# Second norm of a hybrid decoder layer: the gain applied to turned rows by VectorE in halves, the stored rows scaled by ScalarE

## The reference, cut to what matters

```python
def rmsnorm(x, g):
    xf = x.astype(jnp.float32)
    xf = xf * lax.rsqrt(jnp.mean(xf * xf, axis=-1, keepdims=True) + EPS)
    return xf.astype(x.dtype) * g

x = x + merged @ lp['w_out']                      # this is h
x = x + hier_moe(rmsnorm(x, lp['norm2_g']), lp)   # the second norm
...
# hier_moe: router logits from xt, top-1 of 4 groups, then top-2 of 8 experts inside it
for e in range(N_EXPERTS):                        # 32 experts, 1024 -> 256 -> 1024
    h = jax.nn.silu(xt @ lp['w_e_gate'][e]) * (xt @ lp['w_e_up'][e])
    y = y + combine[:, e:e + 1] * (h @ lp['w_e_down'][e])
```

## Time and profile before

| what | value |
|---|---|
| three runs, us | 781.94, 782.52, 783.98; median 782.52 |
| profiled execution | span 783.6 us; its own time outside the span is not on the page |
| PE busy | 741.4 us, 95% |
| VectorE busy | 408.8 us, 52% |
| ScalarE busy | 259.2 us, 33% |
| POOL busy | 74.4 us, 9% |
| moved by DMA | 190.68 MB, mean 243 GB/s |
| mean granted clock of PE | 0.990 |

### The profile page before, as it was taken

How to read it: one execution, slowest core, us unless ns; L and a number is a source line. 1 busy time by engine, 2 the same in 40 slices (tenths; PEclk the granted TensorE clock), 3 DMA queues, 4 the chain that set the end, 5 groups by cost and what they waited for, 6 DMA issues and landing times.

```text
span 783.6 us, 12757 instructions
## 1 busy us (share of the span) xinstructions
PE 741.4 (95%) x5288; PEld 576.0 (74%) x5288; DVE 408.8 (52%) x755; ACT 259.2 (33%) x446; POOL 74.4 (9%) x104
## 2 busy tenths in 40 slices
PE   8999999999999999999999999999999997778884
PEld 7999999999999777899999988885333332323322
DVE  6999839986347785665154386554112111114226
ACT  5662351123486645532442341230111111100113
POOL 0100022001011111000000000011121221111100
PEclk9999999999999999999999999999999999999997
DMA  9578326434238433400260694389999999999994
GB/s 342 202 264 316 109 82 106 118 115 151 102 131 323 162 138 118 182 1 2 108 219 12 222 425 189 128 353 345 419 423 424 418 424 424 419 423 425 422 388 161
DMA packets 38143, 190.68 MB, mean 243 GB/s; under 512 B 5914, under 2 KB 7466, under 8 KB 21864
## 3 DMA queue, kind: packets, MB, share of 16 engines
q1 hardware_dynamic: 23696, 148.22, 47.8%
q0 software_dynamic: 11200, 34.98, 13.4%
q10 hardware_dynamic: 3184, 6.60, 2.3%
HBM read 176.17 MB, written 21.41 MB: 252 GB/s over the span
## 4 chain that ended last, share of the span: by engine, by line
PE 76%; DMA 14%; DVE 5%; ACT 3%; issue 1%; SPq 1%; DVEq 0%; ACTq 0%; POOLq 0%
PE ps L662 72%; DMA sb<-in_wexp 11%; PE ps L676 4%; DMA expert_rows<-sb 2%; DVE sb L2763 1%; DMA sb<-expert_rows 1%; DMA sb<-in_xT 1%; DVE sb L2298 1%; DVE sb L2284 1%; SPq L562 1%; ACT sb L1431 1%; ACT sb L1631 1%; DVE sb L2696 0%; ACT sb L1653 0%; ACT sb L1636 0%
## 5 line engine op out<-in xcount | busy, mean ns | idle before, releaser
L662 PE MATMUL ps<-sr 128*128 128x288 f32 (+3 forms) x2906 | 407.3, 300 | 3.5 <-DVE ps L2701 3.0
L662 PEld LDWEIGHTS ps<-sr 128*128 128x128 f32 (+1 forms) x2906 | 388.1, 188 | 18.6 <-issue 5.6
L662 PE MATMUL ps<-sb 128*64 128x512 f32 (+16 forms) x1984 | 296.9, 429 | 28.7 <-DMA sb<-in_wexp 18.1
L662 PEld LDWEIGHTS ps<-sb 128*64 128x64 f32 (+7 forms) x1984 | 148.0, 148 | 149.8 <-issue 124.7
L2632 DVE SCALAR_TENSOR_TENSOR sb<-sb,ps 128x256 f32<-128x256 f32 x16 | 6.7, 421 | 117.7 <-ACT sb L1830 117.7
L676 PEld LDWEIGHTS ps<-sb 128*128 128x128 f32 (+3 forms) x398 | 42.2, 140 | 31.0 <-issue 28.6
L676 PE MATMUL ps<-sb 128*128 128x128 f32 (+3 forms) x398 | 53.7, 273 | 2.3 <-issue 1.4
L2246 DVE TENSOR_TENSOR sr<-sb,sr 128x2048 fp32r<-128x2048 f32 (+1 forms) x17 | 39.3, 2320 | 29.1 <-ACT sr L1545 19.0
L2640 DVE COPY sb<-ps 128x1024 f32<-128x1024 f32 x15 | 18.4, 1225 | 54.5 <-PE ps L662 54.5
L1431 ACT ACTIVATE sb<-ps 128x576 f32<-128x576 f32 (+3 forms) x28 | 21.9, 783 | 67.4 <-PE ps L662 47.4
L2357 DVE SCALAR_TENSOR_TENSOR sb<-sb,ps 128x576 f32<-128x576 f32 x24 | 18.1, 753 | 46.5 <-PE ps L662 46.3
(11 more groups left out here) (291 smaller groups left out, 509.2 us busy)
## 6 DMA issues: line engine op xcount, KB each, us to landing
sb<-in_wexp SPq DMA_DIRECT2D x91, 1024.0 KB, 22.1
sb<-in_wstream SPq DMA_DIRECT2D x33, 1024.0 KB, 5.7
expert_rows<-sb ACTq DMA_DIRECT2D x1, 4608.0 KB, 24.9
sb<-in_mkT POOLq DMA_DIRECT2D x8, 512.0 KB, 7.7
sb<-in_mv POOLq DMA_DIRECT2D x8, 512.0 KB, 5.1
sb<-expert_rows SPq DMA_DIRECT2D x4, 1024.0 KB, 9.0
sb<-in_wexp SPq DMA_DIRECT2D x5, 768.0 KB, 25.4
sb<-in_x SPq DMA_DIRECT2D x4, 512.0 KB, 14.1
```

What stands on the lines that cost most here:

```text
L662: return signed(nc.tensor.matmul(*a, **kw))
```

## The change

ScalarE writes the stored rows, h times the inverse root, for all five tiles (`scaled_rows`), each one loop step after the tile's sum of squares and ahead of `copy_x2T` of the same tile. VectorE only takes the reciprocals. The gain is applied when the gathered and turned rows leave PSUM; that copy moves from ScalarE to VectorE, in two halves of 512 columns, behind `hidden(i)` and ahead of `result(i-1)`. PE waits for the first half before `gate_up(i,0)` and for the second before `gate_up(i,1)`. The gain row `M_G2`, its load and POOL's product go.

```diff
 # PE
             def gate_up(i, h):
-                if i == 0 and h == 0:
-                    pe.wait_ge(half_sb, 1)
+                if h == 0:
+                    pe.wait_ge(half_sb, i + 1)
                 else:
                     pe.wait_ge(xT_sb, i + 1)
 # ScalarE
+            def scaled_rows(t):
+                R, to = WROWS[t], at(M_X2 + (t % 2) * 1024, (1, D), pn=WROWS[t])
+                act.wait_ge(norm_ready, t + 1)
+                wait_pos(act, x2_out[t % 2], 16 * (t // 2))
+                fn(to, at(H_AT[t], (1, D), pn=R), ACT.Copy, scale=at(R_SS + t, (1, 1), pn=R)).then_inc(x2_ready, 1)
             for t in range(TT):
                 if t == 0:
                     shift(0)
                     shift(2)
                 else:
+                    scaled_rows(t - 1)
                     copy_x2T(t - 1)
 ...
-            act.wait_ge(rs_last, 1)
-            act.wait_ge(x2_gain, 1)
-            last = at(M_X2, (1, D), pn=WROWS[4])
-            fn(last, last, ACT.Copy, scale=at(R_SS + 4, (1, 1), pn=WROWS[4])).then_inc(x2_ready, 1)
+            scaled_rows(TT - 1)
-            def rows_turned(i):
-                act.wait_ge(xt_ps, i + 1)
-                wait_pos(act, gu_ps, i)
-                fn(at(M_XGT, (1, 1024)), pat(PS_X, 0, (1, 1024)), ACT.Copy).then_inc(xT_sb, 1)
 # VectorE
-                c.do(v.reciprocal(ss, ss), rs_last if t == TT - 1 else None)
+                c.do(v.reciprocal(ss, ss), norm_ready)
-            def norm(t):
-                ...
-                c.do(v.scalar_tensor_tensor(at(M_X2 + (t % 2) * 1024, (1, D), pn=R), at(H_AT[t], (1, D), pn=R),
-                                            at(R_SS + t, (1, 1), pn=R), at(M_G2, (1, D), pn=R), ALU.mult, ALU.mult), x2_ready)
+            def turned_half(src, h):
+                return v.tensor_tensor(at(M_XGT + 512 * h, (128, 4), (1, 128)), pat(src, 512 * h, (128, 4), (1, 128)),
+                                       at(M_GT + 4 * h, (1, 4), (0, 128)), ALU.mult)
+            def rows_turned(i):
+                dve.wait_ge(xt_ps, i + 1)
+                wait_pos(dve, gu_ps, i)
+                turned_half(PS_X, 0).then_inc(half_sb, 1)
+                turned_half(PS_X, 1).then_inc(xT_sb, 1)
             def pairs(i0, i1):
                 for i in range(i0, i1 - 1):
                     hidden(i)
+                    rows_turned(i + 1)
                     if i > i0:
                         result(i - 1)
 # POOL
-                    pool.dma_start(at(M_G2, (1, D)), bass.AP(rows.tensor, rows.offset, [[0, P], [1, D]])).then_inc(ld["rows"], 16)
-                if t == TT - 1:
-                    pool.wait_ge(h_ready, 4 * TT)
-                    pool.wait_ge(ld["rows"], 32)
-                    pool.wait_ge(x2_out[0], 32)
-                    nc.gpsimd.tensor_tensor(at(M_X2, (1, D), pn=R), at(H_AT[t], (1, D), pn=R), at(M_G2, (1, D), pn=R),
-                                            ALU.mult).then_inc(x2_gain, 1)
```

More of the change, by code:

```diff
@@ L167 @@
 M_X2T = O_X + 2048
-M_G2, M_WR, M_BR, M_GT = O_TH, O_TH + 2048, O_TH + 2368, O_TH + 2408
+M_WR, M_BR, M_GT = O_TH + 2048, O_TH + 2368, O_TH + 2408
 M_R = O_TH + 2416
@@ L455, in build @@
             sem(n) for n in ("rt_ready", "x2_ready", "x2T_sb", "gate_d", "gate_e", "m_onehot", "oh_ready", "idx_ready"))
-        oh2_ready, rows_ps, over_step, side_ready, wr_ready, rs_last, x2_gain = (
-            sem(n) for n in ("oh2_ready", "rows_ps", "over_step", "side_ready", "wr_ready", "rs_last", "x2_gain"))
+        oh2_ready, rows_ps, over_step, side_ready, wr_ready, norm_ready = (
+            sem(n) for n in ("oh2_ready", "rows_ps", "over_step", "side_ready", "wr_ready", "norm_ready"))
         hi_ready, lo_ready, sel0_ready = sem("hi_ready"), sem("lo_ready"), sem("sel0_ready")
@@ L1833, in pairs @@
             def pairs(i0, i1):
-                if i0:
-                    rows_turned(i0)
                 for i in range(i0, i1):
@@ L1839, in pairs @@
                     gate(i)
-                    if i < i1 - 1:
-                        rows_turned(i + 1)
                 hidden_turned(i1 - 1)
@@ L2522, in select_first @@
                      sel0_ready)
+            def turned_half(src, h):
+                return v.tensor_tensor(at(M_XGT + 512 * h, (128, 4), (1, 128)), pat(src, 512 * h, (128, 4), (1, 128)),
+                                       at(M_GT + 4 * h, (1, 4), (0, 128)), ALU.mult)
             def first_turned():
-                def half(h):
-                    return v.tensor_tensor(at(M_XGT + 512 * h, (128, 4), (1, 128)), pat(pair("xs"), 512 * h, (128, 4), (1, 128)),
-                                           at(M_GT + 4 * h, (1, 4), (0, 128)), ALU.mult)
                 dve.wait_ge(rows_ps, 1)
-                half(0).then_inc(half_sb, 1)
+                turned_half(pair("xs"), 0).then_inc(half_sb, 1)
                 dve.wait_ge(rows_ps, 2)
                 dve.sem_inc(ps_free[pair("xs2")], 1)
-                c.free(half(1), "xs2")
+                c.free(turned_half(pair("xs"), 1), "xs2")
                 c.settle()
@@ L2565, in _ @@
                                  ALU.mult), wr_ready)
-            dve.wait_ge(ld["rows"], 32)
+            dve.wait_ge(ld["rows"], 16)
             for b in (0, 2):
@@ L2575, in _ @@
                     add_h(1, 1)
-                    norm(0)
+                    inverse_norm(0)
                     add_h(2, 1)
@@ L2583, in _ @@
                 select_first(t - 1)
-                if t < TT - 1:
-                    norm(t)
-            inverse_norm(4)
+                inverse_norm(t)
             choose(4)
@@ L2679, in pairs @@
             def pairs(i0, i1):
+                if i0:
+                    rows_turned(i0)
                 for i in range(i0, i1 - 1):
                     hidden(i)
+                    rows_turned(i + 1)
                     if i > i0:
```

## The result

| | before | changed |
|---|---|---|
| median, us (4 runs each) | 782.38 | 787.61 |
| lowest to highest | 781.94 to 783.98 | 786.93 to 788.47 |
| span of the profiled execution | 783.6 | 785.8 (own time 787.58) |

The ratio is 1.0052, with an interval of 1.0038 to 1.0065. The changed kernel was run again in two later sessions, each against the kernel before on the same chip: 1.0022 (1.0011 to 1.0033) and 1.0049 (1.0031 to 1.0067). So it is slower, by 0.2 to 0.5%, that is 1.7 to 4 us; forecast was 1.3 us, and the median is above the range given.

A forecast was written before the change was run, and what follows sets the result against it. PE bounds the kernel until 544 us, then expert-weight transfers at about 420 GB/s. Terms 1.25 (standstill at tile 0's logits) + 0.05 (pair 1) = 1.3 us, added to 782.52, gave 783.8 us; range 781.4 to 785.6 us.

The forecast's parts named there:

- where PE stands still, why and how long: At tile 0's logits, PE waits for a copy queued behind ScalarE's stored rows: 1.07 to 1.40 us, taken as 1.25.
- the terms of 0: Norm products, stored rows of tiles 1 to 4, gain load and later pairs' halves were each forecast to cost or gain 0.
- the 1.70 us: VectorE time freed in place_rows(3) once POOL's product goes; forecast gain 0, or 1.70 us if PE had been waiting.
- the wait of pair 1: PE's wait for turned rows in pair 1 stays about 1.1 us, now released by VectorE; cost taken as 0.05 us.
- the step on tile 4: Tile 4's stored rows start on the same reciprocal, so last store and chunk 19 keep their place relative to PE: 0.
- A microsecond of PE after 544 us costs nothing: Premise for the expert stream: transfers already run at full rate, so PE delays there are free while chunks are under way.
- PE's clock falls too: Rival at tile 0's logits: standstill also brings half clock, 1.7 us more, 785.5 us; chance 0.15.
- The standstill is absorbed: Rival at tile 0's logits: early reciprocal or later routing slack hides the wait, 782.6 us; chance 0.15.
- VectorE becomes late in the pair loop: Rival in the pair loop: halves come late for gate_up, 784.5 to 788 us; chance 0.04.
- the lifted load pays: Rival on VectorE and POOL near 521 us: freed time gives 782.1 us, or 780.4 without the clock fall; chance 0.12.
- The base: Whole-kernel starting time to which the forecast sum was added: the median of the runs, 782.52 us.

The follow-up runs named there:

- r7: Kernel before, with ScalarE waiting for tile 0's reciprocal and writing its rows to a spare buffer ahead of the copy: 785.21 us, 1.0016.
- r3: Kernel before with only the pair loop's part, turned rows in halves on VectorE, gain applied twice: 783.89 us, 1.0004.
- r13: Kernel before with the last store held back by a 512-column ScalarE copy that POOL also waits for: 785.00 us, 1.0018.
- r5: Changed kernel, no edit, in another session against the kernel before: 786.09 us, 1.0022.
- r1: Kernel before, no edit, against itself: 783.80 us, 1.0003.
- r11: Changed kernel with tile 0's copy first and turned rows copied by ScalarE without the gain, so the old pair loop: 784.42 us, 1.0023.
- r12: Changed kernel, no edit, in a further session against the kernel before: 785.88 us, 1.0049, 6 executions.
- r14: Changed kernel with tile 4's rows stored from ScalarE's own queue instead of POOL's: 784.20 us, 1.0004.
- r10: Changed kernel with tile 0's turned tile copied ahead of its stored rows, other tiles as in the change; second session: 783.83 us, 1.0014.
- r4: Changed kernel with turned rows again copied whole by ScalarE, without the gain, leaving the stored rows' part: 786.17 us, 1.0026.
- r8: Changed kernel with ten unread matmuls of 256 columns on PE in front of tile 0's logits: 786.37 us, 1.0020.
- r2: Changed kernel with ScalarE copying the turned tile ahead of the stored rows for all tiles in its loop: 784.97 us, 1.0015.
- r9: Changed kernel with tile 0's copy first, plus gain row, its load and POOL's overwritten tile 4 product put back: 783.86 us, 1.0002.

## Why the prediction was wrong

**Right: where PE stands still, why and how long.** Forecast 1.07 to 1.40 us, taken as 1.25; measured 1.22 us at `logits(0)`, released by ScalarE, in the order of steps that was given. It isn't absorbed later (PE is behind by it at 548 us too). Its share of the time was forecast at its full length, and r7 gives 1.2 us, with an interval of -0.1 to 2.6 us.

**Right: the terms of 0.** Tiles 1 to 3 hide ScalarE's write: the copy of tile 3 still waits for PE, now 0.96 us instead of 2.58. In VectorE's timeline of the changed kernel `place_rows(3)` is back at 0.29 us, and what follows waits for ScalarE instead, so the 1.70 us are worth nothing:

```profile
524.21 0.29 DVE L2498 TENSOR_TENSOR sb<-sb 128x128 f32<-128x128 f32 x1
...
527.52 0.17 DVE L2455 RECIPROCAL sb<-sb 128x1 f32<-128x1 f32 x1 [2.04 <-ACT sb L1815]
```

In the pair loop the wait of pair 1 is 1.05 us (forecast about 1.1), and from pair 2 on the halves are hidden; r3 finds the whole part at 1.0004.

**Wrong: the step on tile 4.** The prediction said of it: "So the last store, and chunk 19 with it, keep their place relative to PE: 0." The store is issued 0.52 us behind ScalarE's rows instead of 0.31, and in 7 of 10 profiles with the new stored rows chunk 19 is issued 9.0 to 9.4 us after the store, in four with the old ones 8.4 to 8.6 us (but 9.06 us in r13). That alone would be 1 us at most. The prediction looked at the store only as the release of chunk 19. It is also the release of the gather of pair 1, and there the kernel before has little in hand: the indices come 0.25 to 0.34 us after the landing. If the landing is the later of the two, the gather lands 7.0 to 7.5 us after its issue instead of 3.4 to 4.5 us, PE runs dry for 2.2 to 2.9 us, and the clock falls for 6.8 us. Up to the end of the stream that costs 4.1 us in r5 and 4.6 us in r13, both against r1. The term that was sized 0 is therefore 0 in some executions and 4 to 5 us in others, and r13 and r11, which have no standstill, put it at 1.3 us each in the means. With the standstill's 1.2 us that is 2.5 us; the means of r5 and r12 are 2.1 and 2.9 us above the kernel before.

A premise failed with it: "A microsecond of PE after 544 us costs nothing". In r13 PE loses a good part of its time at half clock from 544.6 us on, and the stream ends later by it. Behind 655 us the premise holds: r14 has 6.8 us at a granted clock of 0.50 there and still takes 192.6 us from chunk 20 to `down(13)`.

The race at the gather also explains why the profile of the changed kernel shows nothing of it: in that execution the clock fell just ahead of the store's issue, which delays the indices by 1.6 us and so lets the store win. This is the stretch, to set against the first of the earlier trace rows, and below it the place of that first one in r1, with 34 matmuls instead of 18 in the same 3.40 us:

```profile
528.60:532.00 3.40, 3.40 (x17) 3.40 (x18) 2.51 (x15) 1.55 (x2) 0.54 (x1) 0.50 1.01 419
526.20:529.60 3.40, 3.40 (x34) 3.40 (x32) 2.33 (x14) 1.35 (x2) 0.58 (x1) 1.00 1.03 414
```

In r5, r10 and r13 there was no such fall. An execution without it is 1.6 us ahead, and may then lose this and more at the gather: none of the nine profiles with the fall lost the race, and of six without it, with the store on POOL and not held back, r5 and r10 lost it and r1, r4, r7 and r12 didn't. So the kernel before still has good executions (its fastest are 781.4 to 781.6 us), and the changed kernel hardly any (fastest 784.79 us of r5's 12 and 784.22 us of r12's 6).

**The rivals.** "PE's clock falls too" is not what happened: no profile has a stretch at 0.50 that follows the standstill at `logits(0)`, and r8 gains nothing by filling it. Its mechanism came all the same, at another place, behind the 2.8 us of pair 1. The Trainium skill's rule (TensorE: Matmul & The Clock Gate, "What's actually happening"), that recent activity is what keeps the throttle released, agrees with the trace there: 2.22, 2.79 and 2.87 us of idle time were followed by 0.50, the 1.15 us at `logits(0)` were not. It doesn't tell a fall by itself: 2.75 us of idle time that end at 656.8 us in the profile of before were followed by none, and the fall of the earlier trace rows comes behind 3.10 us in which PE was busy throughout. "The standstill is absorbed", "VectorE becomes late in the pair loop" (r3) and "the lifted load pays" are out.

**The base.** I added the sum to a median of three executions, 782.52 us. Larger samples of the kernel before have medians of 783.2 to 784.2 us. That is 1 us of what looks like an error of the sum, and by their ratios r5 and r12 measure the loss as 1.7 and 3.8 us where the first comparison, of four executions each, had 4.1 us. Of that first comparison some 1.5 us stay open: 787.61 us is 4.0 us above the 783.6 us that is the median of the 133 executions, and 2.5 us of it are accounted for.

**What stays open.** Why the store lands 0.4 to 0.8 us later after its issue in most kernels with the new rows: three of them (r2, r4, r12) had it at 8.4 to 8.6 us, r13 has 9.06 us with the old rows, and r9, which is at the time of the kernel before, had 9.2 us. So r9 does not show that POOL's product matters; between it and r10 (1.0014) the intervals overlap. That r14 keeps the standstill and is at 1.0004 speaks for the store as the larger part of the loss, but its interval reaches 1.0025. How often an execution loses the race was not counted, since only one execution of each kernel is profiled; that r13 has 2 of 12 executions above 786 us says that it is less often, or costs less at the end, than was expected.

## What to carry to other kernels

Before an instruction is put ahead of another in an in-order engine, look at when its own input is ready in each step of the loop: here one of five steps, the first, was the exception, and the copy first for tile 0 alone takes it away without moving a store. List everything that a signal releases, not only what it releases on the chain shown: the last store released a chunk and a gather, and the gather had two conditions 0.25 us apart in r1. And when two conditions are that close, one profile shows one outcome; ask for the time of the other outcome too, and compare on 12 executions or more.

## What the runs showed of the hardware that was not expected

- Executions of one unchanged kernel on one chip differ by where the granted clock falls. The profile of before has a fall to 0.50 at 526.2 to 529.6 us, r1, r4, r12 and r14 have none near there, and it costs 1.6 us (72 matmuls take 9.58 us in the earlier trace rows and 7.95 us in r1). The 6.8 us at 655 us in r14, where PE has time in hand, cost nothing that can be seen in the stream. The kernel before ranges from 781.4 to 789.6 us.
- After 2.2 to 2.9 us of idle time ahead of pair 1 PE had a granted clock of 0.50 for 6.8 us in all three profiles. It isn't so everywhere: a wait for chunks of 2.7 to 2.8 us that ends between 654 and 657 us went with 6.8 us at 0.50 in r14, with 3.4 us in r1 and r12 and with none in the profile of before.
- POOL issued the last store 0.31 us after ScalarE's rows where it had run a product until 3.3 us before, and 0.52 us after them where it had been idle for 13.4 to 16.7 us. In the kernel before the store of tile 3, after 14.45 us of idle time, came 0.53 us after VectorE's rows.
- A store of 0.5 MB landed 2.9 us after its issue in an idle stretch of the queues. Beside the stream of chunks it needed 8.4 to 9.4 us before what waits for it started, and from ScalarE's queue 8.6 to 8.9 us.
- A gather of 128 rows beside the stream landed after 3.4 to 4.5 us where the next chunk was issued 1.9 us or more behind it (14 profiles), and after 7.0 to 7.5 us where that was 1.3 to 1.5 us (r5, r10, r13).
